# Gathering residual rows with their inverse root as a column, and building the expert lists in smaller groups

## The chip, the cores and the metric

The kernel runs on one core of one Trainium2 chip. The metric is device time in microseconds (us) of one execution, the median of several runs. Engines are named as the profile names them: PE (TensorE), DVE (VectorE), ACT (ScalarE), POOL (GpSimd), SP (SyncE, which here only issues transfers).

## What is computed

One layer of a hybrid decoder on 520 tokens (512 of a prompt and 8 of a decoding batch), width 2048, all in float32: an RMSNorm and an input projection, a state-space branch and a dilated attention branch, an output projection with a residual add, and then a hierarchical mixture of experts. The change touches only the last part:

```python
def _finish(x, z_ssm, o_attn, lp):
    ...
    x = x + mix @ lp['w_out']                 # called x2 in the kernel
    h = _rmsnorm(x, lp['g_ffn_norm'])
    y = _hier_moe(h.reshape(b * s, D_MODEL), ...)
    return x + y.reshape(b, s, D_MODEL)

def _hier_moe(h, w_rg, b_rg, w_re, b_re, w_g, w_u, w_d):
    # router: best of 4 groups, then the best 2 of its 8 experts
    ...
    def expert_block(args):
        rows, e = args
        xb = h_pad[rows]
        return (jax.nn.silu(xb @ w_g[e]) * (xb @ w_u[e])) @ w_d[e]
    ...
    out = jax.ops.segment_sum(contrib, tok_s, num_segments=t)
```

There are 32 experts with 3 weight matrices of 4 MB each, so 403 MB of weights are read by the expert stage alone. A last RMSNorm gives the output.

## The kernel before

All engines run one program each, written out by hand, with semaphores between them. The stages follow each other: projections, scan and attention (to 758 us), the output projection of 16 column tiles (758 to 996 us), the router with its lists (1003 to 1051 us), 32 experts (1051 to 2115 us), the last norm.

**Rows of x2.** After every four tiles of the output projection PE turns them into token rows, ACT copies these to the tile `x2row` and squares them for the norm, and SP stores them to the DRAM tensor `x2_rows` (`store_x2`). When the last tile is in, the square root and its reciprocal give the inverse root of each row (`row_rstd`). ACT then multiplies all five row tiles by it (L1078), SP stores them to a second DRAM tensor `h_rows` (L519), and POOL starts gathering rows for the experts from `h_rows` once all five stores have landed (`s_hst`).

**Routing.** DVE computes logits, the two experts of each token and, from PE's prefix sums (L799), each token's position in its expert's list. It ranks the experts by their token counts (L1545 to L1551: `key`, `place`, `turn_of`); experts 0 and 1 are always the first two. The six first in the order are "wide" (128 list slots), the others "narrow" (64); what doesn't fit goes into up to 16 overflow blocks. After the ranking DVE computes for every token its block and its slot (`posblk`, `rv16`). A one-hot comparison (`select`, L1612) and small fp16 matmuls on PE (`lists`, L812) turn these into the index lists `idx_g` and `idx_s`. There are seven groups of lists: `GROUPS` holds first block, last block and slots.

**Experts.** Six halves of weights (2 MB each: gate, up, gate, up, down, down) are loaded per expert into a ring of ten slots by SP, in order; they are counted here from 0, so expert i uses the halves 6i to 6i+5. Slots 8 and 9 lie in region `A`, which also holds x2 and then the scratch of the routing. For each expert PE does `gate_up`, then `turn_rows` (transposes of the next expert's gathered rows), `turn_act`, `down`. A slot is loaded again only when PE has used the half that lies in it:

```python
def load_next(n, e):

    if n >= NSLOT:
        i, j = divmod(n - NSLOT, 6)
        if j < 2:
            sp.wait_ge(s_half, i + 1)
        elif j < 4:
            sp.wait_ge(s_up, i + 1)
        elif j == 4:
            sp.wait_ge(s_dh, i + 1)
        else:
            sp.wait_ge(s_dn, 2 * i + 2)
    load_half(n % NSLOT, n % 6, e)
```

Here `s_half` counts the experts whose first gate and up halves are used, `s_up` those whose `gate_up` is done, `s_dh` the first down halves used, `s_dn` two for each `down`.

On PE the first three groups of lists stand ahead of expert 0, the other four between its `gate_up` and the turning of expert 1's rows. On SP the halves 0 to 3 are loaded during the output projection, 4 to 6 after it, 7 when the stores to `h_rows` have landed, and 8 when all lists are done (`s_idx`). POOL gathers the rows of expert i+2 when those of expert i have been turned, then scatters the result rows of expert i.

Of the kernel before, what the change touches and what calls it, by code (L numbers as in the profile page):

```python
# [24 lines left out]
P = 128  # L25
# [15 lines left out]
GROUPS = [(0, 6, CAP), (6, 15, SLIM), (15, 24, SLIM), (24, 32, SLIM), (32, 38, CAP), (38, 44, CAP), (44, 48, CAP)]  # L41
LISTG = 9
# [28 lines left out]
def build(nc, t):  # L71
    at = layout()
    ctx = ExitStack()
    with ctx:
# [17 lines left out]
        h_rows = dram("h_rows", (T, DM))  # L92
        x2_rows = dram("x2_rows", (T, DM))
# [80 lines left out]
        xrow = [view(ms + DM * j, DM) for j in range(2)]  # L174
        xtr = view(ms + 4096, 16 * CAP)
        actv = view(ms + 6144, 512)
        actt = view(ms + 6656, 4 * CAP)
        yrow = view(ms + 7168, DM)
# [63 lines left out]
        s_hr = sem("h_row_ready")  # L242
        s_x2st, s_hst = sem("x2_stored"), sem("h_stored")
        s_lg = sem("logits_psum")
        s_ra, s_rb = sem("router_act"), sem("router_dve")
        s_pos = sem("positions_psum")
        s_sel, s_lst, s_idx = sem("selection_ready"), sem("lists_psum"), sem("indices_ready")
# [35 lines left out]
        keep = Cols(ms + 7168 + DM)  # L283
        gate_w = keep(10).rearrange("p (t j) -> p t j", t=5)
        idx_g = keep(NBLK).bitcast(U32)
        idx_s = keep(NBLK).bitcast(U32)
        idx_now = keep(2).bitcast(U32)
# [4 lines left out]
        assert keep.at <= ring0, keep.at - ring0  # L292
        late = Cols(at["rstd"])
# [4 lines left out]
        rt = Cols(at["A"])  # L298
        SELN = 5 * 6 * CAP // 2
        sel_at = rt.at  # L300
        sel_v = [rt(SELN), rt(SELN), yrow[:, 0:SELN]]
        order_t = [view(sel_at + NE * NE * j, NE * NE).rearrange("p (a b) -> p a b", a=NE) for j in range(2)]

        def sel16(g):
            b0, b1, cap = GROUPS[g]
            n = 5 * (b1 - b0) * cap // 2
            return sel_v[g % 3][:, 0:n].bitcast(F16).rearrange("p (t b s) -> p t b s", t=5, b=b1 - b0)

        wide_at = rt.at
# [4 lines left out]
        wide_e = [view(wide_at, 320), view(wide_at + 320, 320), rt(320), rt(320)]  # L314
# [9 lines left out]
        none = rt(2 * LISTG)  # L324
# [50 lines left out]
        TURNED = [sum(TURNS[:i]) for i in range(NE + 1)]  # L375

# [7 lines left out]
        def _(sp):  # L384
# [87 lines left out]
            def store_x2(g):  # L472

                c = slice(512 * g, 512 * (g + 1))
                sp.wait_ge(s_trev, 5 * (g + 1))
                sp.dma_start(x2_rows[0:SEQ, c].rearrange("(i p) n -> p i n", p=P), x2row[:, 0:4, c]
                             ).then_inc(s_x2st, 16)
                sp.dma_start(x2_rows[SEQ:T, c], x2_of[4][0:NS, c]).then_inc(s_x2st, 16)

# [24 lines left out]
            for n in range(2, 16):  # L504
                if n % 4 == 3 and n > 4:
                    store_x2(n // 4 - 1)
# [4 lines left out]
            store_x2(3)  # L511
# [12 lines left out]
            for n in range(8, 12):  # L524
                load_next(n, 1)
            sp.wait_ge(s_ord, 1)
# [15 lines left out]
            for i, n in enumerate(TOKS):  # L542
                sp.dma_start(fx[i][0:n], x2_rows[P * i:P * i + n, :]).then_inc(s_finl[i], 16)
# [13 lines left out]
            sp.wait_ge(s_hst, 16 * 5)  # L557
# [3 lines left out]
        def _(pe):  # L561
# [242 lines left out]
            def lists(g):  # L804
# [3 lines left out]
                if g >= 3:  # L808
                    pe.wait_ge(s_idx, g - 2)
                for b in range(b1 - b0):  # L810
                    for i in range(5):
                        last = mm(ps[0:cap, 4 + g % 3, 2 * b:2 * b + 2], sel16(g)[:, i, b, :],  # L812
                                  rv16[:, i, b0 + b, :], start=(i == 0), stop=(i == 4))
                last.then_inc(s_lst, 1)

            def turn_rows(j, gathered, cap, turned):

                pe.wait_ge(s_gat[j], gathered)
                rows = xrow[j][0:cap, :].rearrange("p (m k) -> p k m", k=16)
# [71 lines left out]
            for g in range(3):  # L891
                lists(g)
            turn_rows(0, 16, CAP, 0)
            for i in range(NE):
                slots, uses = slots_of(i)
                gate_up(WIDE[i], slots, uses, TURNED[i + 1], i)
                if i == 0:
                    for g in range(3, len(GROUPS)):
                        lists(g)
                if i + 1 < NE:  # L900
                    turn_rows((i + 1) % 2, 16 * ((i + 1) // 2 + 1), CAP if WIDE[i + 1] else SLIM, TURNED[i + 1])
                turn_act(WIDE[i], i)
                if i == 0:
                    pe.wait_ge(s_idx, len(GROUPS))
                down(WIDE[i], slots, uses, i)

            def overflow_block(it):
                turned = it * 4 + TURNED[NE]
                turn_rows(0, it * 16 + 16 * (NE // 2 + 1), CAP, turned)
# [9 lines left out]
        def _(act):  # L919
# [143 lines left out]
            for b in range(20):  # L1063
# [52 lines left out]
        def _(pool):  # L1116
# [103 lines left out]
            pool.wait_ge(s_hst, 16 * 5)  # L1220
# [21 lines left out]
        def _(dve):  # L1242
# [246 lines left out]
            dve.wait_ge(s_rrs, 2)  # L1489
            dve.wait_ge(s_lg, 1)  # L1490
# [39 lines left out]
            p_, b_, w_, o_, id_, q_, f_, over_ = C10[0:8]  # L1530
# [3 lines left out]

            dve.wait_ge(s_pos, 1)
# [15 lines left out]
            dve.tensor_copy(ord_i, turn_of).then_inc(s_ord, 1)  # L1551
            link(ts(room, place, float(NWIDE), float(CAP - SLIM), ALU.is_lt, ALU.mult))
# [53 lines left out]
            def select(g):  # L1606
                b0, b1, cap = GROUPS[g]
                if g == 2:
                    dve.wait_ge(s_hst, 16 * 5)
                if g >= 3:  # L1610
                    dve.wait_ge(s_lst, g - 2)
                tt(sel16(g), iota_s[:, 0:cap].unsqueeze(1).unsqueeze(1).to_broadcast([P, 5, b1 - b0, cap]),  # L1612
                   posblk[:, :, b0:b1].unsqueeze(3).to_broadcast([P, 5, b1 - b0, cap]),
                   ALU.is_equal).then_inc(s_sel, 1)

            def lists(g):
# [221 lines left out]
```

## Time and profile before

| | |
|---|---|
| median of 3 runs | 2178.23 us (2176.87 to 2182.03) |
| the profiled execution | 2177.13 us, of which the profile's span is 2175.3 us |
| busy share of the span | PE 85%, DVE 27%, ACT 13%, POOL 12% |
| read from DRAM, written | 522.81 MB, 37.26 MB |
| mean granted TensorE clock | 0.933 |
| DMA engines busy, by fortieths of the span | 5143122257634034325199999999999999999947 |

Each digit of the last line is a tenth of busy time in a slice of 54 us: the transfers fill the expert stage, and there is a hole right before it. Times in the rows below are in us from the span's start, unless marked otherwise.

### The profile page before, as it was taken

The numbers are of one execution on the slowest core, as the hardware profiler recorded it, in microseconds if no ns is written. First come the engines' busy times: TensorE is split into PE (matmuls) and PEld (weight loads), VectorE is DVE, ScalarE is ACT, GpSimd is POOL, SyncE is SP. The second block draws the span as 40 slices with busy tenths as digits, with TensorE's granted clock in tenths as the row PEclk, the third lists the DMA queues.
The fourth block names the chain that finished last, engine by engine and source line by source line (L and its number), as shares of the span: only waits on it lengthen the run. The fifth ranks groups of instructions, "written<-read, shape, count | busy, mean of one in ns | idle before, by whom it ended". The sixth has DMA issues, their size and how long they took to land.

```text
span 2175.3 us, 22268 instructions
## 1 busy us (share of the span) xinstructions
PE 1848.2 (85%) x8916; PEld 1158.4 (53%) x8916; DVE 594.2 (27%) x1115; ACT 271.9 (13%) x535; POOL 270.6 (12%) x187
## 2 busy tenths in 40 slices
PE   7798999998789899994899896988979877877870
PEld 6687888886467688883443332433334332332320
DVE  6800799642144300005611111010110100100116
ACT  3001211004531101113000000000000000000002
POOL 0641222203900000000100000010000000000000
PEclk9899999999989999997799998999999998988995
DMA  5143122257634034325199999999999999999947
GB/s 222 59 135 98 65 77 77 104 197 137 4 137 178 36 116 170 122 78 214 53 400 397 392 409 408 407 412 393 398 412 386 391 413 406 411 400 406 399 203 295
DMA packets 91141, 544.85 MB, mean 250 GB/s; under 512 B 27984, under 2 KB 40784, under 8 KB 44400
## 3 DMA queue, kind: packets, MB, share of 16 engines
q1 hardware_dynamic: 70512, 520.24, 63.1%
q0 software_dynamic: 5888, 17.05, 2.3%
q10 hardware_dynamic: 14656, 6.33, 1.3%
q8 instruction: 64, 1.05, 0.2%
q14 instruction: 21, 0.17, 0.0%
HBM read 522.81 MB, written 37.26 MB: 257 GB/s over the span
## 4 chain that ended last, share of the span: by engine, by line
PE 58%; DMA 25%; DVE 9%; POOL 3%; ACT 2%; issue 1%; SPq 1%; ACTq 0%; POOLq 0%; DVEq 0%
PE psum L567 30%; DMA arena<-w_up_in 22%; PE psum L884 9%; PE psum L849 7%; PE psum L842 4%; PE psum L845 3%; PE psum L825 2%; DMA arena<-y_rows 1%; DMA arena<-v_cache_in 1%; DVE arena L1612 1%; SPq L484 1%; PE psum L729 1%; DVE arena L1709 1%; PE psum L765 1%; DVE arena L1450 1%
## 5 line engine op out<-in xcount | busy, mean ns | idle before, releaser
L567 PE MATMUL psum<-arena 128*128 128x260 f32 x3328 | 750.5, 389 | 40.3 <-ACT arena L930 13.4
L567 PEld LDWEIGHTS psum<-arena 128*128 128x128 f32 x3328 | 642.7, 194 | 144.1 <-issue 29.0
L849 PE MATMUL psum<-arena 128*64 128x512 f32 x832 | 402.5, 642 | 115.6 <-DMA arena<-w_up_in 115.6
L851 PE MATMUL psum<-arena 128*64 128x512 f32 x832 | 403.2, 643 | 0.0
L849 PEld LDWEIGHTS psum<-arena 128*64 128x64 f32 x832 | 119.5, 148 | 379.7 <-issue 379.7
L884 PE MATMUL psum<-arena 128*64 128x512 f32 (+1 forms) x1024 | 275.3, 606 | 17.7 <-ACT arena L1095 17.0
L884 PEld LDWEIGHTS psum<-arena 128*64 128x64 f32 (+1 forms) x1024 | 95.6, 149 | 174.8 <-issue 152.7
L1210 POOL DMA_INDIRECT y_rows<-arena x32 | 30.0, 938 | 998.3 <-DVE arena L1686 998.3
L1677 DVE TENSOR_TENSOR arena<-arena,psum 64x512 f32<-64x512 f32 x26 | 18.0, 691 | 495.4 <-ACT arena L1092 495.4
L1686 DVE COPY arena<-psum 64x512 f32<-64x512 f32 (+1 forms) x64 | 43.5, 687 | 280.6 <-PE psum L884 279.8
L851 PEld LDWEIGHTS psum<-arena 128*64 128x64 f32 x832 | 119.5, 148 | 0.0
L842 PE MATMUL psum<-arena 128*128 128x512 f32 x192 | 86.6, 604 | 4.9 <-DMA arena<-w_up_in 4.1
L845 PE MATMUL psum<-arena 128*128 128x512 f32 x192 | 84.4, 592 | 0.0
L1092 ACT ACTIVATE arena<-psum 64x512 f32<-64x512 f32 x26 | 15.3, 589 | 511.2 <-PE psum L849 511.2
L825 PEld LDWEIGHTS psum<-arena 64*128 64x128 f32 (+1 forms) x512 | 62.6, 204 | 30.2 <-issue 24.1
L825 PE MATMUL psum<-arena 64*128 64x64 f32 (+1 forms) x512 | 69.6, 287 | 4.2 <-DVE arena L1634 4.0
L1483 DVE TENSOR_TENSOR arena<-psum,arena 128x520 f32<-128x520 f32 x16 | 11.2, 700 | 223.0 <-PE psum L567 223.0
L1355 DVE TENSOR_TENSOR arena<-arena 128x64 f32<-128x64 f32 x128 | 46.3, 361 | 92.7 <-ACT arena L959 82.3
L1101 ACT ACTIVATE arena<-psum 64x512 f32<-64x512 f32 (+1 forms) x64 | 37.3, 593 | 248.4 <-PE psum L884 247.7
L842 PEld LDWEIGHTS psum<-arena 128*128 128x128 f32 x192 | 36.6, 193 | 53.4 <-issue 52.2
L845 PEld LDWEIGHTS psum<-arena 128*128 128x128 f32 x192 | 36.5, 190 | 45.9 <-issue 45.9
L1222 POOL MEMSET arena<- 128x2048 f32 x2 | 3.5, 1804 | 436.1 <-DMA h_rows<-arena 436.1
(309 smaller groups left out, 1348.2 us busy)
## 6 DMA issues: line engine op xcount, KB each, us to landing
arena<-w_gate_in SPq DMA_DIRECT2D x64, 2048.0 KB, 38.2
arena<-w_up_in SPq DMA_DIRECT2D x64, 2048.0 KB, 42.3
arena<-w_down_in SPq DMA_DIRECT2D x64, 2048.0 KB, 41.6
arena<-w_in_in SPq DMA_DIRECT2D x32, 1024.0 KB, 4.8
arena<-w_out_in SPq DMA_DIRECT2D x16, 1024.0 KB, 4.8
arena<-k_cache_in SPq DMA_DIRECT2D x8, 1024.0 KB, 6.8
arena<-v_cache_in SPq DMA_DIRECT2D x8, 1024.0 KB, 4.8
arena<-y_rows SPq DMA_DIRECT2D x4, 2048.0 KB, 19.3
```

What stands on the lines that cost most here:

```text
L484: sp.dma_start(half_gu(slot), src[:, 8 * (j // 2):8 * (j // 2) + 8, :]).then_inc(s_ring[slot], 16)
L567: last = mm(pair(n)[:, h, :], w(kk), rhs(kk)[:, HALF * h:HALF * (h + 1)], start=(kk == 0), stop=(kk == kn - 1 and stop))
L825: last = pe.transpose(ps[:, g % 2, cap * m:cap * (m + 1)], rows[:, per * g + m, :], ident[0:cap, 0:cap])
L842: lastg = mm(ps[:, 2, :], xt[:, 8 * hf + kk, :], wg[:, kk, :], start=(hf == 0 and kk == 0), stop=(hf == 1 and kk == 7))
L845: lastu = mm(ps[:, 3, :], xt[:, 8 * hf + kk, :], wu[:, kk, :], start=(hf == 0 and kk == 0), stop=(hf == 1 and kk == 7))
L849: lastg = mm(ps[0:SLIM, 2, :], xt[:, 8 * hf + kk, :], wg[:, kk, :], start=(hf == 0 and kk == 0), stop=(hf == 1 and kk == 7))
L851: lastu = mm(ps[SLIM:P, 2, :], xt[:, 8 * hf + kk, :], wu[:, kk, :], start=(hf == 0 and kk == 0), stop=(hf == 1 and kk == 7))
L884: last = mm(out, at_[:, kk, :], wd[:, kk - 2 * hf, 512 * c:512 * (c + 1)], start=(kk == 0), stop=(kk == 3))
L1101: A(yrow[0:cap, 512 * c:512 * (c + 1)], src, ACT.Copy).then_inc(s_ya, 1)
L1210: pool.indirect_dma_start(out=y_rows, out_offset=bass.IndirectOffsetOnAxis(ap=index, axis=0), in_=yrow[0:cap, :], in_offset=None, bounds_c ...
L1355: tt(scan_t[:, 0], column(it * 4 + s), lam_same, ALU.mult).then_inc(s_scan, 1)
L1686: dve.tensor_copy(yrow[0:cap, 512 * c:512 * (c + 1)], src).then_inc(s_yd, 1)
```

## The change

- `h_rows`, ACT's multiplication and SP's five stores go. `x2_rows` gets 16 more columns (`ROWW` = 2064), all holding the row's inverse root: DVE spreads it over 16 columns, ACT stores them in five small transfers. POOL gathers rows of 2064 from `x2_rows`, and DVE multiplies the gathered rows by their last column (`scale_rows`) ahead of the turning.
- The stores of x2 move from SP to ACT.
- On SP the halves 4 to 8 wait until all stores have landed; half 8 no longer waits for the lists. The halves 10 and 11 go ahead of 9; half 9 waits until the routing's scratch is free (`s_free`).
- The scratch of the routing moves into the slot of half 9; lists and list scratch that live longer move elsewhere.
- The lists of experts 0 and 1 (a group of its own, blocks 0 to 1) are made ahead of the ranking. The ranking, expert 0's scaling and the turning of its rows follow; the rest of the routing comes behind those on DVE. Two more groups (`EARLY` = 3 in all) are made into lists on PE and DVE after expert 0's `gate_up`, behind the turning of expert 1's rows; the other 25 groups (two narrow blocks or one overflow block each) are made two at a time behind the first 13 experts.

```diff
-GROUPS = [(0, 6, CAP), (6, 15, SLIM), (15, 24, SLIM), (24, 32, SLIM), (32, 38, CAP), (38, 44, CAP), (44, 48, CAP)]
+EARLY = 3
+GROUPS = ([(0, 2, CAP), (6, 15, SLIM), (2, 6, CAP)] + [(b, min(b + 2, NE), SLIM) for b in range(15, NE, 2)]
+          + [(b, b + 1, CAP) for b in range(NE, NBLK)])
+ROWW = DM + 16
...
-        h_rows = dram("h_rows", (T, DM))
-        x2_rows = dram("x2_rows", (T, DM))
+        x2_rows = dram("x2_rows", (T, ROWW))
...
+        LATE = (len(GROUPS) - EARLY + 1) // 2
...
             sp.wait_ge(s_op, 16)
+            sp.wait_ge(s_x2st, 16 * 8)
+            sp.wait_ge(s_rst, 16 * 5)
             for n in range(4, 6):
                 load_next(n, 0)
             load_next(6, 1)
-            for i, n in enumerate(TOKS):
-                sp.wait_ge(s_hr, i + 1)
-                sp.dma_start(h_rows[P * i:P * i + n, :], x2_of[i][0:n]).then_inc(s_hst, 16)
-            sp.dma_start(gtab, t["g_ffn"].rearrange("o (p k) -> (o p) k", k=16)).then_inc(s_gt, 16)
-            sp.wait_ge(s_hst, 16 * 5)
+            sp.wait_ge(s_rss, 20)
             load_next(7, 1)
-            sp.wait_ge(s_idx, len(GROUPS))
-            for n in range(8, 12):
+            sp.wait_ge(s_lg, 1)
+            load_next(8, 1)
+            for n in (10, 11):
                 load_next(n, 1)
+            sp.wait_ge(s_free, 1)
+            load_next(9, 1)
             sp.wait_ge(s_ord, 1)
...
+            def late_lists(i):
+                for g in range(EARLY + 2 * i, min(EARLY + 2 * i + 2, len(GROUPS))):
+                    lists(g, ps[:, 0, 8 * (g % 2):8 * (g % 2) + 8])
...
-                pe.wait_ge(s_gat[j], gathered)
+                pe.wait_ge(s_sr, scaled)
...
-            for g in range(3):
-                lists(g)
-            turn_rows(0, 16, CAP, 0)
+            lists(0, ps[:, 4, :])
+            turn_rows(0, 1, CAP, 0)
             for i in range(NE):
                 slots, uses = slots_of(i)
                 gate_up(WIDE[i], slots, uses, TURNED[i + 1], i)
+                if i + 1 < NE:
+                    if 1 <= i <= LATE:
+                        pe.wait_ge(s_idx, min(EARLY + 2 * i, len(GROUPS)))
+                    turn_rows((i + 1) % 2, i + 2, CAP if WIDE[i + 1] else SLIM, TURNED[i + 1])
                 if i == 0:
-                    for g in range(3, len(GROUPS)):
-                        lists(g)
-                if i + 1 < NE:
-                    turn_rows((i + 1) % 2, 16 * ((i + 1) // 2 + 1), CAP if WIDE[i + 1] else SLIM, TURNED[i + 1])
+                    for g in range(1, EARLY):
+                        lists(g, ps[:, 4 + g, :])
                 turn_act(WIDE[i], i)
                 if i == 0:
-                    pe.wait_ge(s_idx, len(GROUPS))
+                    pe.wait_ge(s_idx, EARLY)
                 down(WIDE[i], slots, uses, i)
+                if i < LATE:
+                    if i + 1 < NE:
+                        pe.wait_ge(s_xte, TURNED[i + 2])
+                    late_lists(i)
...
+                if i == 4:
+                    c = slice(512 * g, 512 * (g + 1))
+                    act.dma_start(x2_rows[0:SEQ, c].rearrange("(i p) n -> p i n", p=P), x2row[:, 0:4, c]
+                                  ).then_inc(s_x2st, 16)
+                    act.dma_start(x2_rows[SEQ:T, c], x2_of[4][0:NS, c]).then_inc(s_x2st, 16)
...
-            act.wait_ge(s_rrs, 2)
-            act.wait_ge(s_x2st, 16 * 8)
+            act.wait_ge(s_rsc, 1)
             for i, n in enumerate(TOKS):
-                A(x2_of[i][0:n], x2_of[i][0:n], ACT.Copy, scale=row_rstd[0:n, i:i + 1]).then_inc(s_hr, 1)
+                act.dma_start(x2_rows[P * i:P * i + n, DM:ROWW], rstd_cols[0:n, i, :]).then_inc(s_rst, 16)
...
-                    out=xrow[j][0:cap, :], out_offset=None, in_=h_rows,
+                    out=xrow[j][0:cap, :], out_offset=None, in_=x2_rows,
...
-            pool.wait_ge(s_hst, 16 * 5)
+            pool.wait_ge(s_x2st, 16 * 8)
+            pool.wait_ge(s_rst, 16 * 5)
...
+            dve.tensor_copy(rstd_cols, row_rstd.unsqueeze(2).to_broadcast([P, 5, 16])).then_inc(s_rsc, 1)
...
+            tt(two(first_a), hot1[:, :, 0:2], full(id_[:, 0:5], 2), ALU.mult)
+            link(tt(two(first_b), hot2[:, :, 0:2], full(id_[:, 5:10], 2), ALU.mult))
+            tt(rv16[:, :, 0:2, 0:1], two(first_a).unsqueeze(3), two(first_b).unsqueeze(3), ALU.add)
+            link(dve.tensor_copy(rv16[:, :, 0:2, 1:2], full(tok1, 2).unsqueeze(3)))
...
             dve.wait_ge(s_pos, 1)
+            link(stt(posblk[:, :, 0:2], ps[:, 1, 0:160].rearrange("p (t e) -> p t e", t=5)[:, :, 0:2], 1.0,
+                     m16[:, :, 0:2], ALU.add, ALU.mult))
+            select(0)
             link(dve.tensor_copy(rank, ps[:, 1, 0:160].rearrange("p (t e) -> p t e", t=5)))
             link(dve.tensor_copy(cnt, ps[:, 1, 160:192]))
+            lists(0, ps[:, 4, :])
+            dve.wait_ge(s_x2st, 16 * 8)
...
             dve.tensor_copy(ord_i, turn_of).then_inc(s_ord, 1)
...
+            def scale_rows(j, gathered, cap):
+                dve.wait_ge(s_gat[j], gathered)
+                ts(xrow[j][0:cap, 0:DM], xrow[j][0:cap, 0:DM], xrow[j][0:cap, DM:DM + 1], None, ALU.mult
+                   ).then_inc(s_sr, 1)
+
+            dve.wait_ge(s_gt, 16)
+            scale_rows(0, 16, CAP)
+            rows_turned(CAP, 0)
             link(ts(room, place, float(NWIDE), float(CAP - SLIM), ALU.is_lt, ALU.mult))
...
-            select(0)
-            lists(0)
             select(1)
-            select(2)
-            lists(1)
-            lists(2)
-            dve.wait_ge(s_gt, 16)
-            rows_turned(CAP, 0)
-
             dve.wait_ge(s_ra, 4)
...
-            for g in range(3, len(GROUPS)):
+            select(2)
+            for g in range(EARLY, EARLY + 2):
                 select(g)
-                if g >= 5:
-                    lists(g - 2)
-            for g in range(len(GROUPS) - 2, len(GROUPS)):
-                lists(g)
...
             for i in range(NE):
+                if i + 1 < NE:
+                    scale_rows((i + 1) % 2, 16 * ((i + 1) // 2 + 1), CAP if WIDE[i + 1] else SLIM)
                 gated(i, WIDE[i])
                 if i + 1 < NE:
                     rows_turned(CAP if WIDE[i + 1] else SLIM, TURNED[i + 1])
+                if i == 0:
+                    for g in range(1, EARLY):
+                        lists(g, ps[:, 4 + g, :])
+                    dve.sem_inc(s_free, 1)
                 rows_out(i, WIDE[i])
+                if i < LATE:
+                    dve.wait_ge(s_lst, min(EARLY + 2 * i + 2, len(GROUPS)))
+                for g in range(EARLY + 2 * i, min(EARLY + 2 * i + 2, len(GROUPS))):
+                    lists(g, ps[:, 0, 8 * (g % 2):8 * (g % 2) + 8])
+                for g in range(EARLY + 2 * i + 2, min(EARLY + 2 * i + 4, len(GROUPS))):
+                    select(g)
```

## Rows read from the trace of the kernel before

**Rows 1.** Busy time by stretch: instructions in brackets, granted clock, DMA share, GB/s.

```profile
1003.00:1037.00 34.00, 2.92 (x63) 2.58 (x63) 29.19 (x82) 13.87 (x13) 2.47 (x2) 0.51 0.90 354
...
1042.00:1087.00 45.00, 41.88 (x278) 24.23 (x278) 25.72 (x41) 0.60 (x1) 3.46 (x2) 0.84 0.07 16
...
1087.00:2107.00 1020.00, 877.13 (x3597) 354.52 (x3595) 110.98 (x166) 67.99 (x125) 57.08 (x60) 0.94 0.98 395
```

**Rows 2.** The chain that ended last, in order of time, its last wait for weights.

```profile
2055.40 42.16 DMA arena<-w_up_in
```

**Rows 3.** SP's issues in order of time: start, length, line, destination and source.

```profile
1004.18 1.80 SPq L487 DMA_DIRECT2D arena<-w_down_in  x2
...
1010.62 7.86 SPq L519 DMA_DIRECT2D h_rows<-arena  x5
...
1034.50 0.33 SPq L484 DMA_DIRECT2D arena<-w_up_in  x1
1086.64 0.33 SPq L484 DMA_DIRECT2D arena<-w_gate_in  x1
...
1152.22 0.33 SPq L484 DMA_DIRECT2D arena<-w_up_in  x1
1159.25 0.95 SPq L487 DMA_DIRECT2D arena<-w_down_in  x2
```

**Rows 4.** All engines in order of time, from the router to expert 0.

```profile
1008.59 9.57 ACT L1078 ACTIVATE arena<-arena 128x2048 f32<-128x2048 f32 x5 [4.01 <-DMA x_rows<-arena]
...
1012.31 0.32 DVE L1528 TENSOR_TENSOR arena<-arena 128x160 f16<-128x160 f32 x1
...
1020.70 0.17 DVE L1552 TENSOR_SCALAR arena<-arena 128x32 f32<-128x32 f32 x1
...
1031.96 4.16 DVE L1612 TENSOR_TENSOR arena<-arena 128x3840 f16<-128x3840 f32 x1
...
1034.53 3.54 POOL L1222 MEMSET arena<- 128x2048 f32 x2 [436.12 <-DMA h_rows<-arena]
...
1037.53 0.15 DVE L1624 SCALAR_TENSOR_TENSOR arena<-psum,arena 128x6 uint32<-128x6 f32 x1
...
1039.09 2.90 POOL L1201 DMA_INDIRECT arena<-h_rows,arena  x1 [1.01 <-issue]
...
1040.93 2.56 PE L812 MATMUL psum<-arena 128*64 128x2 f16 x45 [3.72 <-DVE arena L1612]
...
1046.49 3.97 PE L825 MATMUL psum<-arena 128*128 128x128 f32 x16
...
1051.24 8.80 PE L842 MATMUL psum<-arena 128*128 128x512 f32 x16 [0.78 <-DVE arena L1634]
...
1056.25 10.96 DVE L1612 TENSOR_TENSOR arena<-arena 128x2560 f16<-128x2560 f32 x3
```

**Rows 5.** PE after expert 0's gate and up products, in order of time.

```profile
1080.57 3.01 PE L812 MATMUL psum<-arena 128*64 128x2 f16 x100
...
1091.55 15.97 PE L884 MATMUL psum<-arena 128*128 128x512 f32 x32 [0.73 <-issue]
```

**Rows 6.** The 32 gathers: duration on POOL and landing, each as minimum, median and maximum.

```profile
L1201 POOL DMA_INDIRECT arena<-h_rows,arena x32: 949/955/2905, 1039.1 to 2027.9; - x32
...
DMA to landing us min/median/max: 5.2/11.9/17.1
```

**Rows 7.** Landing of single transfers: gather 0, half 8 (issued 1086.64), half 22 (1159.25).

```profile
arena<-h_rows,arena POOLq DMA_INDIRECT x1, 6.1
...
arena<-w_gate_in SPq DMA_DIRECT2D x1, 2048.0 KB, 7.4
...
arena<-w_down_in SPq DMA_DIRECT2D x1, 2048.0 KB, 15.1
```

**Rows 8.** DVE by line and shape: busy, mean ns of one.

```profile
L1612 DVE TENSOR_TENSOR arena<-arena 128x2880 f16<-128x2880 f32 x2 | 6.2, 3154 | 0.0
...
L1285 DVE TENSOR_SCALAR arena<-arena 128x1056 f32<-128x1056 f32 x1 | 0.7, 709 | 0.0
```

More of the change, by code:

```diff
@@ L172, in build @@
         ro_at = at["cos"]
[L174 to L178, printed above, removed]
+        xrow = [view(ms + ROWW * j, ROWW) for j in range(2)]
+        xtr = view(ms + 2 * ROWW, 16 * CAP)
+        actv = view(ms + 2 * ROWW + 2048, 512)
+        actt = view(ms + 2 * ROWW + 2560, 4 * CAP)
+        yrow_at = ms + 2 * ROWW + 3072
+        yrow = view(yrow_at, DM)
         ring = [ring0 + HALFW * j for j in (4, 5, 6, 7, 1, 2, 3, 0)] + [at["A"], at["A"] + HALFW]
@@ L296, in build @@
         assert late.at <= at["cos"]
[L298 to L302, printed above, removed]
+        none = stat[:, 44:62]
+        rstd_cols = region("lr", 80).rearrange("p (t c) -> p t c", t=5)
+        late_sel = [view(ro_at + 30, 320), region("lr", 320)]
+        rt = Cols(at["A"] + HALFW)
+        scratch_at = rt.at
+        order_t = [yrow[:, NE * NE * j:NE * NE * (j + 1)].rearrange("p (a b) -> p a b", a=NE) for j in range(2)]
+        early_sel = [view(scratch_at, 640), yrow[:, 0:1440], view(scratch_at, 1280)]
         def sel16(g):
@@ L556, in _ @@
             sp.wait_ge(s_vout, 16)
-            sp.wait_ge(s_hst, 16 * 5)
+            sp.wait_ge(s_x2st, 16 * 8)
+            sp.wait_ge(s_rst, 16 * 5)
         @block.tensor
@@ L1533, in _, with two, select, lists @@
             link(ts(tok1, tok, 1.0, None, ALU.add))
+            def two(ap):
+                return ap.rearrange("p (t b) -> p t b", t=5)
+            tt(two(first_a), hot1[:, :, 0:2], full(id_[:, 0:5], 2), ALU.mult)
+            link(tt(two(first_b), hot2[:, :, 0:2], full(id_[:, 5:10], 2), ALU.mult))
+            tt(rv16[:, :, 0:2, 0:1], two(first_a).unsqueeze(3), two(first_b).unsqueeze(3), ALU.add)
+            link(dve.tensor_copy(rv16[:, :, 0:2, 1:2], full(tok1, 2).unsqueeze(3)))
+            def select(g):
+                b0, b1, cap = GROUPS[g]
+                if g >= EARLY + 2:
+                    dve.wait_ge(s_lst, g - 1)
+                tt(sel16(g), iota_s[:, 0:cap].unsqueeze(1).unsqueeze(1).to_broadcast([P, 5, b1 - b0, cap]),
+                   posblk[:, :, b0:b1].unsqueeze(3).to_broadcast([P, 5, b1 - b0, cap]),
+                   ALU.is_equal).then_inc(s_sel, 1)
+            def lists(g, out):
+                b0, b1, cap = GROUPS[g]
+                dve.wait_ge(s_lst, g + 1)
+                src = out[0:cap, 0:2 * (b1 - b0)].rearrange("p (b c) -> p b c", c=2)
+                no = none[0:cap, 0:2 * (b1 - b0)].rearrange("p (b c) -> p b c", c=2)
+                link(ts(no, src, 0.0, BIG, ALU.is_equal, ALU.mult))
+                stt(idx_s[0:cap, b0:b1].unsqueeze(2), src[:, :, 0:1], -1.0, no[:, :, 0:1],
+                    ALU.add, ALU.add)
+                stt(idx_g[0:cap, b0:b1].unsqueeze(2), src[:, :, 1:2], -1.0, no[:, :, 1:2],
+                    ALU.add, ALU.add).then_inc(s_idx, 1)
+                dve.wait_ge(s_idx, g + 1)
             dve.wait_ge(s_pos, 1)
+            link(stt(posblk[:, :, 0:2], ps[:, 1, 0:160].rearrange("p (t e) -> p t e", t=5)[:, :, 0:2], 1.0,
+                     m16[:, :, 0:2], ALU.add, ALU.mult))
+            select(0)
             link(dve.tensor_copy(rank, ps[:, 1, 0:160].rearrange("p (t e) -> p t e", t=5)))
             link(dve.tensor_copy(cnt, ps[:, 1, 160:192]))
+            lists(0, ps[:, 4, :])
+            dve.wait_ge(s_x2st, 16 * 8)
             def across(ap):
@@ L1551, in _, with rows_turned @@
             dve.tensor_copy(ord_i, turn_of).then_inc(s_ord, 1)
+            def rows_turned(cap, turned):
+                per = 512 // cap
+                xt = xtr[:, 0:16 * cap].rearrange("p (k n) -> p k n", k=16)
+                for g in range(16 // per):
+                    dve.wait_ge(s_xt, turned + (g + 1))
+                    tt(xt[:, per * g:per * (g + 1), :], ps[:, g % 2, :].rearrange("p (k n) -> p k n", n=cap),
+                       gtab[:, per * g:per * (g + 1)].unsqueeze(2).to_broadcast([P, per, cap]), ALU.mult
+                       ).then_inc(s_xte, 1)
+            def scale_rows(j, gathered, cap):
[5 more added lines that the diff above has]
+            rows_turned(CAP, 0)
             link(ts(room, place, float(NWIDE), float(CAP - SLIM), ALU.is_lt, ALU.mult))
```

81 lines of the change are left out of this document (23 added, 58 removed).

## Prediction

> **What bounds the kernel now.** I read the page's busy slices first, then the stretches, the chain, SP's issues and the order of work around the router. The slices show transfers filling the second half of the span with a hole before it. The stretches give both sizes: from 1087 to 2107 us the DMA engines are busy 0.98 of the time, and from 1042 to 1087 they are busy 0.07 of it [rows 1]. The chain says the same from the other end: its last wait for weights is 42.16 us long and ends at 2097.6 [rows 2]. So the expert stage is a stream of 192 halves that has no slack: halves 8 to 189, 182 of them, land between 1086.64 [rows 3] and 2097.6, 5.55 us each, 33 us an expert. Its end moves only if the stream gets ahead earlier, or if each expert costs the stream something else.
>
> SP's issues tell why it starts so late. Halves 4 to 6 go out at 1004 to 1006, half 7 only at 1034.50, when the `h_rows` stores have landed, half 8 at 1086.64, when all lists are done [rows 3]. POOL's memset began at 1034.53 for the same reason, and expert 0 at 1051.24 [rows 4]. But the hole of 45 us is not the gain to be had. A ring of ten slots lets halves 16 and later go only as PE frees them, so after the hole the stream can't run ahead of PE. I look for the place where both meet: half 22 (expert 3's first down half), issued at 1159.25 when expert 2's first half was used, and landed 15.1 us later, at 1174.4 [rows 3, 7]. A half with nothing ahead of it took 7.4 us [rows 7], so 7.7 us of that were queue: there the stream was behind PE, and it stays full to the end.
>
> **The change part by part.** Times after are on the scale of the trace before.
>
> *Stores and root column.* ACT's two issues for the last rows stand ahead of the square root. An issue on SP took 0.33 us [rows 3]; for ACT I take 0.5, of which the old wait for DVE's sum hides a part: 0.8 us. DVE's copy into 16 columns is a short operation, 0.2. The selected experts (`m16`), ready at 1012.6 before [rows 4], come at 1013.6. Between none and twice these prices lies 1 us to either side.
>
> *List 0.* Seven short DVE operations, four of them new, and the position read follow, at 0.17 us [rows 4] and a gap 0.2 each, with PE's sums beside them: 1015.2. The selection has 2 x 5 x 128 = 1280 elements; 3840 took 4.16 us [rows 4], so 1.4: 1016.6. PE's 10 matmuls, where 45 took 2.56 [rows 4], 0.6; three DVE operations, 0.6: list 0 at 1017.8. Before, the first list ended at 1037.68 and the gather started at 1039.09 [rows 4], 1.4 later: 1019.2. On ACT only the two exponentials for the gates stand behind the new issues, and DVE reads those after expert 0 has started. The stores don't hold the gather: those of x2 landed at 1008.6 before [rows 4], the five root columns some 3 us later, and POOL's memset of 3.54 [rows 4] then ends near 1015.5.
>
> *Gather 0.* Before, it took 6.1 us beside the end of one half [rows 7], of which POOL's first issue was 2.9 where the others took 0.96 [rows 6]. Now SP sends the halves 4 to 8 once the stores have landed, near 1011.5, five times some 5 us, until about 1037, so the gather meets them. Under the full stream the 32 gathers had a median of 11.9 and a maximum of 17.1 [rows 6]. I take the median and the longer first issue, 11.9 + 1.9 = 13.8: it lands at 1033.0. The ends are 6.1 (1025.3) and 17.1 + 1.9 (1038.2).
>
> *Scaling and turning.* One DVE operation of 2048 elements; 1056 took 0.71 [rows 8], so at most 1.4; I take 1.3. The lower end is the 0.7 of half as many elements, the upper the pace of the selection in the same rows, 2.2. PE's turning up to expert 0's first product took 1046.49 to 1051.24 [rows 4], 4.75. Expert 0 starts at 1039.1 instead of 1051.24: **12.1 us earlier**.
>
> *What waits behind it on DVE.* The scaling stands in DVE's queue ahead of the rest of the routing, 1020.70 to 1031.96 = 11.3 us [rows 4]; select 1, 3.15 [rows 8]; gates and overflow, 1051.24 to 1056.25 = 5.0 [rows 4]; select 2, 2.8; two of 640 elements, 1.4; expert 1's scaling, 1.3. Together 25 us, hidden behind expert 0's gate and up products, 1051.24 to 1080.57 = 29.3 [rows 4, 5]. Cover of 4 us is left; beyond it each us of DVE holds expert 1's turning by one.
>
> *After expert 0's products.* Before, PE came to the down product 11.0 us after them [rows 5], waiting for selections. Now: turning 4.0 [rows 4], lists of 45 and 20 matmuls 2.6 + 1.1, the turning of the activations a quarter of 4.0, ACT's copy 0.6: 9.3, so 1.7 gained. Each later pair of lists is 20 matmuls, 1.1 us on PE; two pairs stand before expert 2. Expert 2 starts 12.1 + 1.7 - 2.3 = **11.5 us earlier**. The remaining pairs fall into experts that wait for weights, and cost nothing while they do.
>
> *The halves.* Half 8 leaves early; 10 and 11 wait for expert 0's first half; 9 waits behind them on SP for the scratch, near 1077, with 12 and 13 right after it. All three are there by about 1094, and half 9 is needed in the middle of expert 1, after 1107. From 14 on PE sets the issues: during two wide experts pairs of halves, 10 us of stream, go out every 14 us or so, so the queue runs empty. Half 21, issued at 1152.22 before [rows 3], goes 12.7 earlier, at 1139.5, and lands 7.4 later, before half 22 is issued at 1159.25 - 11.5 = 1147.8. What half 22 can still meet is expert 1's scatter and gather. With none of the old queue it lands 11.5 + 7.7 = 19.2 earlier, with all of it 11.5; since only one expert's row transfers stand there, for which I allow 2 us, I take **17**.
>
> *The rest of the stream* is as full as before, so the 17 us last to the end. DVE's scalings of later experts wait for gathers, but a gather is issued about an expert (33 us) ahead and lands 17.1 at the latest [rows 6]. They stand ahead of `gated`, which waits for PE's whole product anyway. The tail after the last weights is untouched.
>
> The profiled execution took 2177.13 (span 2175.3), 1.1 under the median. So 2177.1 - 17 = 2160.1 on its scale, **2161 us** as a median.
>
> **Rivals.** *Gather 0 lands as on an empty queue* (it has few rows and goes out while the halves have just begun): 1025.3, the start 7.7 earlier still, gain 24.7, 2153.5. For it: its own 6.1 before; against: five halves in flight, and the median of 11.9 among full queues [rows 6].
>
> *The early start is taken back: the gather waits out the halves sent ahead of it.* Before, the gather started with one half in flight; now with five. If it landed only after all of them, near 1039 to 1045, expert 0 would start at 1045 to 1051 and the gain be 11 to 5: 2167 to 2173. It decides from a landing at 1045, 26 us after issue. Against it: of the 32 gathers, nearly all in the full stream, none took over 17.1 [rows 6]. The Trainium skill (DMA: Bandwidth & Descriptors, "Queues, rings and completion order") says that each DMA engine takes turns between queues packet by packet; by that rule the gather would not wait out the halves, and the trace's 17.1 agrees.
>
> *Slower: each expert costs the full stream more.* Rows are 64 bytes longer and no longer start at a multiple of 8 KB, and DVE now works 1.3 us per expert on the tile that POOL's gathers fill. With no slack in the stream, 17 us over 30 experts is gone at 0.57 us an expert; at the whole 1.3 us it would be 39 - 17 = 22 slower, 2199. Against it: the bytes grow by 0.8% of the gathers, and the weights, nearly all of the stream, are issued by SP, not POOL. The Trainium skill (SBUF — State Buffer, "SBUF: two separate sides") warns of this: an fp32 copy-like DVE operation in a two-port mode locks GpSimd out of its SBUF port, so that descriptors of POOL's transfers are written only after it. By that rule up to 1.3 us per expert would be added to a gather; no run here shows whether the stream feels it.
>
> **How the numbers follow.** The forecast has 0.58, with its own range from 2155 to 2168 (landing of the gather 5.2 either way, queue 2). The empty-queue rival has 0.12, the lost start 0.16, the slower one 0.10; 0.04 is left for what I don't see. The range runs from 2150, a few us below the empty-queue case, to 2173, the worst of the lost start, and leaves the slower case out. A measurement of this kernel tells 0.3%, 6.5 us, from no change: under 2171.7 is faster. That takes the first two and three quarters of the lost start: 0.82. The rest of it, and part of the unseen, is the same: 0.08. Slower 0.10.
>
> **What would show it.** In the profile after: expert 0's first product near 1039 (right if 1033 to 1045); gather 0's landing 14 us after its start; the DMA share between 1042 and 1087 well over 0.07; half 22 issued near 1148 and landing within 10 us; the stretch from half 22 to the last weights as long as before. The prediction is wrong if that stretch grows, by 0.57 us an expert or more, if DVE's routing ends after expert 0's products, or if expert 0 starts after 1051.

## The result and the profile after

The changed kernel takes **2150.07 us** (median of 4 runs, 2146.59 to 2152.12) against 2177.77 of the kernel before beside it (4 runs, 2176.87 to 2182.03). The ratio is 0.9871, 95% interval 0.9859 to 0.9884: 27.7 us faster. The forecast was 2161, a gain of 17: the direction was right, the size was not. The time lies outside the forecast's own range (2155 to 2168) and on the edge of the whole one (2150 to 2173).

The profiled execution took 2152.12 us, its span 2150.5. One thing has to be settled before its rows are set beside those of before. The position sums of PE, up to which both kernels do nearly the same work, stand at different times:

```profile
1012.69 0.72 PE L799 MATMUL psum<-arena 128*128 128x32 f16 x20 [8.22 <-DVE arena L1528]
```

(the kernel before, PE in order of time), and after:

```profile
1015.79 0.72 PE L798 MATMUL psum<-arena 128*128 128x32 f16 x20 [8.43 <-DVE arena L1541]
```

Of the 3.1 us, 2.8 are older than the change: the output projection's first matmuls begin at 758.15 before and at 760.91 here, and in the nine profiled executions of this kernel and those below, whose code is the same up to there, at 757.5 to 762.8. From there to the sums it is 254.5 us before and 254.7 to 254.9 in the nine, so what the change adds ahead of the sums costs at most 0.3. So times below are compared **after the sums**, as distances from these two rows and their like. On that scale the profiled execution is 24.8 + 3.1 = 27.9 us shorter, as the medians say.

The stretches, with the columns of [rows 1]:

```profile
1012.00:1037.00 25.00, 4.54 (x45) 3.91 (x46) 16.15 (x37) 1.88 (x4) 6.97 (x4) 0.50 0.98 399
1042.00:1087.00 45.00, 43.71 (x169) 21.32 (x168) 23.90 (x53) 1.19 (x2) 0.95 (x1) 0.92 0.57 213
1087.00:2070.00 983.00, 855.88 (x3682) 348.75 (x3680) 169.83 (x288) 66.45 (x122) 71.46 (x60) 0.94 0.99 398
```

The hole of 45 us, 0.07 busy before [rows 1], is now 0.57 busy, and the stream behind it is as full as it was. SP's issues tell which halves fill it (4 to 8 go out at 1011.79 to 1014.19, then 10 and 11 together, 9, and half 22):

```profile
1052.19 0.89 SPq L485 DMA_DIRECT2D arena<-w_down_in  x2
1071.38 0.34 SPq L482 DMA_DIRECT2D arena<-w_up_in  x1
...
1142.28 1.50 SPq L485 DMA_DIRECT2D arena<-w_down_in  x2
```

All engines from list 0 to expert 0's down product, which answer to [rows 4, 5]:

```profile
1011.82 3.57 POOL L1234 MEMSET arena<- 128x2064 f32 x2 [410.32 <-DMA x_rows<-arena]
...
1016.82 1.49 DVE L1561 TENSOR_TENSOR arena<-arena 128x1280 f16<-128x1280 f32 x1
...
1019.24 0.15 DVE L1573 SCALAR_TENSOR_TENSOR arena<-psum,arena 128x2 uint32<-128x2 f32 x1
...
1020.38 1.63 POOL L1212 DMA_INDIRECT arena<-x_rows,arena  x1 [4.99 <-DVE arena L1573]
...
1032.24 1.29 DVE L1612 TENSOR_SCALAR arena<-arena 128x2048 f32<-128x2048 f32 x1 [6.12 <-DMA arena<-x_rows,arena]
1033.58 3.80 PE L827 MATMUL psum<-arena 128*128 128x128 f32 x16 [14.72 <-DVE arena L1612]
1038.16 7.13 PE L844 MATMUL psum<-arena 128*128 128x512 f32 x16 [0.79 <-DVE arena L1606]
...
1065.73 1.06 PE L827 MATMUL psum<-arena 128*128 128x128 f32 x8
1067.35 1.31 PE L827 MATMUL psum<-arena 128*128 128x128 f32 x8 [0.55 <-DVE arena L1606]
1068.59 2.17 PE L809 MATMUL psum<-arena 128*64 128x2 f16 x65
1071.99 17.02 PE L886 MATMUL psum<-arena 128*128 128x512 f32 x32 [0.73 <-DVE arena L1573]
```

Expert 0 begins 22.37 us after the sums, before 1051.24 - 1012.69 = 38.55: 16.2 us earlier. And the landings, gather 0 and half 22, which answer to [rows 7]:

```profile
arena<-x_rows,arena POOLq DMA_INDIRECT x1, 11.8
...
arena<-w_down_in SPq DMA_DIRECT2D x1, 2048.0 KB, 9.3
```

Half 22 is issued 126.49 us after the sums (before 146.56) and lands at 135.79 (before 161.66): 25.9 us earlier. The last transfer of weights in the chain,

```profile
2030.58 40.44 DMA arena<-w_up_in
```

ends at 2030.58 + 40.44 = 2071.02, 1055.2 after the sums, where [rows 2] give 1084.9: 29.6 us earlier. The tail is 1.8 us longer (79.5 against 77.7).

### The profile page after: what moved, and what is told of

Its sections match the earlier page's. It is cut to its first block, busy times and chain, and to the rows that moved or that the text cites. A ratio compares the mean times of both kernels' runs of the same rounds, so it can differ in the third digit from the quotient of the medians.

```text
span 2150.5 us, 22432 instructions
## 1 busy us (share of the span) xinstructions
PE 1849.8 (86%) x8916; PEld 1159.5 (54%) x8916; DVE 644.2 (30%) x1237; ACT 262.4 (12%) x530; POOL 283.1 (13%) x187
## 4 chain that ended last, share of the span: by engine, by line
PE 61%; DMA 23%; DVE 8%; POOL 3%; ACT 2%; issue 1%; SPq 1%; ACTq 0%; POOLq 0%; DVEq 0%
PE psum L566 30%; DMA arena<-w_up_in 20%; PE psum L886 9%; PE psum L851 6%; PE psum L844 4%; PE psum L847 4%; PE psum L853 2%; PE psum L827 2%; DMA arena<-y_rows 1%; DMA arena<-v_cache_in 1%; SPq L482 1%; PE psum L728 1%; DMA arena<-x_rows,arena 1%; DVE arena L1746 1%; PE psum L764 1%
## 5 line engine op out<-in xcount | busy, mean ns | idle before, releaser
L1221 POOL DMA_INDIRECT y_rows<-arena x32 | 36.6, 1144 | 939.0 <-DVE arena L1710 611.5
```

The lines of the kernel that those rows point to most:

```text
L1221: pool.indirect_dma_start(out=y_rows, out_offset=bass.IndirectOffsetOnAxis(ap=index, axis=0), in_=yrow[0:cap, :], in_offset=None, bounds_c ...
```

## The experiments

Three theories were at stake. The *start* (A): the end follows from when expert 0 begins. The *early fill* (B): it follows from the halves that get into the hole. The *ring* (C), formed after the first four runs: a slot is free only when PE has used it, so the stream runs just so far ahead of PE; expert 0's start sets when PE's slots come free, the early halves decide how much has piled up by then, and what fits into the hole costs nothing. C has a gauge, the prediction's own: where half 22 lands, its issue (PE) plus the queue that it meets (halves sent late). Each kernel is the changed one with the edit shown (`...` marks lines left out), and computes all of the reference. Gains are (1 - ratio) x 2177; the ratios' intervals leave 3 to 6 us to either side.

**Scaling on ACT.**

```diff
-            scale_rows(0, 16, CAP)                     # DVE, and one ahead of each gated()
+                act.wait_ge(s_gat[j], gathered)        # ACT, ahead of each expert()
+                A(xrow[j][0:cap, 0:DM], xrow[j][0:cap, 0:DM], ACT.Copy, scale=xrow[j][0:cap, DM:DM + 1]
+                  ).then_inc(s_sr, 1)
```

> The changed kernel, but the gathered rows are multiplied by their root column on ACT instead of DVE. My theory: DVE's scaling does lengthen POOL's issues (mean 1.21 us against 0.97 before), but the stream of weights does not feel it. POOL's gathers go back to about 0.97 us; ACT's operation takes about 2.0 us instead of DVE's 1.3, so expert 0 starts about 0.7 us later; the end stays within 2 us of the changed kernel (2149 to 2152 us). Rival: the lock costs the full stream what it costs POOL, 0.24 us a gather and 0.19 us a scatter over some 28 experts, 12 us; then this kernel is 8 to 12 us faster than the changed one, near 2140 us.

2149.41 us, ratio 0.9864 [0.984, 0.9888]: no difference from the changed kernel; the interval ends at 6.7 us faster, short of the rival's 8 to 12. POOL's gathers and scatters, by line from 1087 us on, were lengthened by DVE's scaling and are nearly not so here. The changed kernel:

```profile
L1221 POOL DMA_INDIRECT y_rows<-arena x32 | 36.6, 1144 | 939.0 <-DVE arena L1710 611.5 <-DVE arena L1573 327.5
L1212 POOL DMA_INDIRECT arena<-x_rows,arena x29 | 35.7, 1232 | 8.8 <-issue 8.8
```

and with the scaling on ACT:

```profile
L1234 POOL DMA_INDIRECT y_rows<-arena x32 | 32.5, 1016 | 949.4 <-DVE arena L1717 613.9 <-DVE arena L1586 335.6
L1225 POOL DMA_INDIRECT arena<-x_rows,arena x29 | 29.5, 1018 | 8.8 <-issue 8.8
```

Before, the same rows had a mean of 939 and 964 ns. So DVE's scaling does lengthen POOL's issues, by some 0.2 us in the mean (12 of the 29 gathers take 1.4 to 1.7 us, the others 0.95 to 1.03 as before), and the full stream does not feel it. Whether a port is what they share was not tried.

**Halves 8, 10 and 11 wait with 9 for the scratch.**

```diff
-            load_next(8, 1)
-            for n in (10, 11):
-                load_next(n, 1)
             sp.wait_ge(s_free, 1)
-            load_next(9, 1)
+            for n in range(8, 12):
+                load_next(n, 1)
```

> The changed kernel, but the halves 8, 10 and 11 wait with 9 until the routing's scratch is free (as they waited for the lists before); nothing else moves. Theory A: the end follows PE's start of expert 2, since halves from 16 on are issued as PE frees slots; three halves more, 15 us of stream, are waiting at 1071 us, but the stream has gaps of some 10 us between there and half 22, so half 22 lands 4 to 6 us later and the end is 4 to 6 us later, 2154 to 2156 us; expert 0 to 2 start as in the changed kernel. Theory B: the gain comes from loading into the hole, so three halves fewer at that point cost 15 us: 2165 us.

2165.91 us, ratio 0.9933 [0.9908, 0.9958]: about half the gain is gone. Expert 0 begins 22.15 us after the sums and half 22 is issued 126.36 after them, both as in the changed kernel,

```profile
1012.34 0.72 PE L796 MATMUL psum<-arena 128*128 128x32 f16 x20 [8.40 <-DVE arena L1539]
...
1034.49 7.13 PE L842 MATMUL psum<-arena 128*128 128x512 f32 x16 [0.78 <-DVE arena L1604]
```

but half 22 lands 18.1 us after its issue, not 9.3:

```profile
arena<-w_down_in SPq DMA_DIRECT2D x1, 2048.0 KB, 18.1
```

A falls: PE ran alike, and the end came 13.5 us later, where A had 4 to 6. B is near, with 13.5 of its 15 us.

**Halves 4 to 6 ahead of the wait for the stores.**

```diff
-            sp.wait_ge(s_x2st, 16 * 8)
-            sp.wait_ge(s_rst, 16 * 5)
             for n in range(4, 6):
                 load_next(n, 0)
             load_next(6, 1)
+            sp.wait_ge(s_x2st, 16 * 8)
+            sp.wait_ge(s_rst, 16 * 5)
```

> The changed kernel, but the halves 4 to 6 are issued as soon as the output projection is done, ahead of the stores' landing, as before; 7 and 8 still wait for the stores. Theory A (end follows PE's start): the five root columns now share the DMA engines with 6 MB of weights and land 3 to 12 us later; POOL's memset and gather 0 follow if they land after 1017 us, and the gather itself meets one or two halves less; expert 0 starts 0 to 8 us later and the end moves by as much: 2150 to 2158 us. Theory B (early fill of the ring decides): halves 4 to 8 are in 5 to 7 us earlier, the end is the same or earlier by up to 5 us: 2145 to 2150 us.

2156.16 us, ratio 0.989 [0.9862, 0.9917]: some 4 us slower than the changed kernel, though the two intervals overlap. That is within A's 2150 to 2158 and above B's 2145 to 2150. The halves don't help by being early; they hold up the stores, and with them POOL:

```profile
1021.43 3.57 POOL L1234 MEMSET arena<- 128x2064 f32 x2 [420.97 <-DMA x_rows<-arena]
```

That is 6.6 us after the sums, where the changed kernel's memset stands 4.0 before them. Expert 0 begins 3.5 us later than there.

**List 0 behind the ranking and the routing.**

```diff
-            select(0)                       # with its four operations, right behind the sums
-            lists(0, ps[:, 4, :])
...
-            dve.wait_ge(s_gt, 16)           # right behind the ranking
-            scale_rows(0, 16, CAP)
-            rows_turned(CAP, 0)
...
+            select(0)                       # behind the ranking and the routing
+            lists(0, ps[:, 4, :])
             select(1)
+            dve.wait_ge(s_gt, 16)
+            scale_rows(0, 16, CAP)
+            rows_turned(CAP, 0)
```

> The changed kernel, but the list of experts 0 and 1 is made after the ranking and the whole routing, as before; root column, stores, early halves and late lists stay. Theory A (end follows PE's start): list 0 comes 18 to 20 us later, near 1040 us instead of 1019; the gather then finds few halves in flight and lands in 6 to 8 us; expert 0 starts 14 to 17 us later than in the changed kernel, near 1053 us, and the end comes 14 to 17 us later: 2164 to 2167 us. Theory B (early fill decides): half 8 is loaded as early as in the changed kernel and only 9 to 11 are late, so no more than 5 us are lost: 2150 to 2155 us.

2164.6 us, ratio 0.9933 [0.9907, 0.9958]. Here A is right and B falls: expert 0 begins 35.62 us after the sums,

```profile
1012.77 0.71 PE L798 MATMUL psum<-arena 128*128 128x32 f16 x20 [8.38 <-DVE arena L1541]
...
1048.39 7.13 PE L844 MATMUL psum<-arena 128*128 128x512 f32 x16 [0.78 <-DVE arena L1593]
```

13.2 us later than in the changed kernel, and the end comes 13.5 later. So each theory explains one of the two runs and fails at the other. That is where C comes from.

**Halves 4 to 8 wait for gather 0.**

```diff
             sp.wait_ge(s_rst, 16 * 5)
+            sp.wait_ge(s_gat[0], 16)
             for n in range(4, 6):
```

> SP holds the halves 4 to 8 until gather 0 has landed, so the gather meets no weights. It took 11.8 us among them; beside the end of one half it took 6.1, so expert 0 should start some 5.7 us earlier, and so should everything that PE releases (halves 10 and 11, then 9, 12 and 13, down to half 22). The halves 4 to 8 are sent some 15 us later, into a hole of the stream that the ring leaves open anyway. Theory C (the ring lets the stream run only so far ahead of PE; transfers that fit into the hole cost nothing): about 5.5 us faster than the changed kernel, 2143 to 2146. Rival (what counts is how early the first halves are in): 2150 to 2158, as the stream has moved nothing for 15 us.

2142.67 us, ratio 0.984 [0.9825, 0.9854]: 6.8 us faster than the changed kernel, the best version of all; C's range was 2143 to 2146, its rival's 2150 to 2158. Its gather 0:

```profile
arena<-x_rows,arena POOLq DMA_INDIRECT x1, 5.0
```

and its engines in order of time:

```profile
1024.29 0.89 SPq L485 DMA_DIRECT2D arena<-w_down_in  x2
1024.78 0.18 DVE L1599 CAST arena<-arena 128x32 uint32<-128x32 f32 x1
1024.87 1.28 DVE L1613 TENSOR_SCALAR arena<-arena 128x2048 f32<-128x2048 f32 x1
...
1030.61 7.13 PE L845 MATMUL psum<-arena 128*128 128x512 f32 x16 [0.89 <-DVE arena L1607]
```

Alone, the gather lands in 5.0 us instead of 11.8; expert 0 begins 6.4 us earlier and the end comes 6.8 earlier, though SP's five halves go out 13.7 us later (9.7 us after the sums, against 4.0 ahead of them). Little more is to be had this way: the rows are in at 1024.2, and the scaling follows the ranking, which ends at 1024.96, without a gap.

**Two stores of 2 MB put back, behind half 8.**

```diff
             load_next(8, 1)
+            for j in (2, 3):
+                sp.wait_ge(s_ring[j], 16)
+                sp.dma_start(extra[P * (j - 2):P * (j - 1), :], view(ring[j], HALFW)).then_inc(s_ext, 16)
             for n in (10, 11):
...
             load_next(9, 1)
+            sp.wait_ge(s_ext, 32)
```

> Two extra stores of 2 MB each (4.2 MB, as much as the five stores to the second row tensor that the change removed) go out on SP behind half 8; nothing but the loads of halves 12 and 13 waits for them. At the stream's 395 GB/s they are 10.6 us of DMA time. Theory C (they fall into the hole of some 15 us between half 8 and half 10): 0 to 2 us, 2150 to 2152. Rival (the stream is one sum of bytes, so the removed stores are 10.6 us of the 27.7 gained): 2158 to 2161.

2150.07 us, ratio 0.9871 [0.9854, 0.9887]: no difference, as C had it. In the stretch after half 8 the DMA engines, busy 0.27 in the changed kernel,

```profile
1036.00:1046.00 10.00, 9.21 (x26) 4.44 (x25) 8.77 (x33) 0.00 (x0) 0.00 (x0) 0.94 0.27 114
```

are busy 0.99 with the extra stores:

```profile
1034.50:1044.50 10.00, 9.22 (x25) 4.40 (x24) 8.69 (x33) 0.00 (x0) 0.00 (x0) 0.93 0.99 401
```

So 4 MB more cost nothing where the stream has a hole. (The stores that the change removed stood elsewhere, ahead of gather 0; what their absence is worth, the last run tells.)

**Halves 10 and 11 behind 9.**

```diff
-            for n in (10, 11):
-                load_next(n, 1)
             sp.wait_ge(s_free, 1)
-            load_next(9, 1)
+            for n in range(9, 12):
+                load_next(n, 1)
```

> The halves 10 and 11 wait with half 9 for the routing's scratch again, so they go out at about 1071 instead of 1052; half 8 stays early, PE's work is untouched. PE theory (the end follows from expert 0's start): 2150. Theory C: two halves, 11.1 us of stream, leave the hole; the holes of some 6 us that the changed kernel's stream still has between 1087 and 1140 are filled by them, so about 5 us slower, 2154 to 2157. Rival (all of the two halves is lost): 11 us, 2161.

2158.03 us, ratio 0.9903 [0.9886, 0.9921], 7.0 us slower than the changed kernel by the ratios: at the upper edge of what C gives (4 to 7; the median lies 1 us above its range) and less than the rival's 11. Half 22 lands 13.8 us after its issue.

**List 0 late and the halves held, together.**

The edits of the second and the fourth run, together.

> Both at once: list 0 is made behind the ranking and the routing (expert 0 starts 13.3 us later, 13.6 us slower by itself), and half 8 is held together with 10, 11 and 9 (13.5 us slower by itself, with expert 0's start as in the changed kernel). What is left of the change is the missing second store of rows and the lists behind the experts. Theory C (with the halves held, the stream is full from the moment the scratch comes free, and that moment moves with expert 0): the two losses add up, 2176 to 2180, the kernel before. Rival (each is a bound by itself and the later one sets the end): 2165 to 2168. Rival (stores and later lists are worth something by themselves, some 10 us): 2168 to 2172.

2177.48 us (12 runs), ratio 1.0 [0.9986, 1.0013]: the whole gain is gone. 13.5 and 13.5 add up to 27.0, and 28.1 were lost. So the missing second tensor of rows, the lists behind the experts and the scaling on DVE bring nothing by themselves, within 3 us and taken together (effects that cancel are not excluded); they are what lets list 0 and the halves go early. (Its profiled execution is 7.4 us shorter after the sums than that of before, which the ratio does not bear out; single executions differ by several us.)

The gauge for all kernels: expert 0's start and half 22's issue in us after the sums, the time from that issue to the landing, and by how much the landing is earlier than before (advance), beside the measured gain:

| kernel | expert 0 | half 22 issued | landing | advance | gain |
|---|---|---|---|---|---|
| before | 38.55 | 146.56 | 15.1 | | |
| changed | 22.37 | 126.49 | 9.3 | 25.9 | 28.1 |
| scaling on ACT | 22.77 | 126.80 | 9.6 | 25.3 | 29.6 |
| halves held | 22.15 | 126.36 | 18.1 | 17.2 | 14.6 |
| halves first | 25.90 | 129.94 | 9.5 | 22.2 | 23.9 |
| list late | 35.62 | 139.92 | 9.5 | 12.2 | 14.6 |
| gather 0 first | 15.98 | 120.02 | 9.2 | 32.4 | 34.8 |
| stores back | 22.20 | 126.41 | 9.6 | 25.7 | 28.1 |
| 10, 11 behind 9 | 21.71 | 126.15 | 13.8 | 21.7 | 21.1 |
| late and held | 35.44 | 139.86 | 17.6 | 4.2 | 0.0 |

From 0 to 34.8 us the gain follows the landing of one half within some 4 us. Neither the start alone nor the queue alone does that: the kernels "halves held" and "list late" have one gain at starts 13.5 us apart. What is left over has a pattern. Where half 8 goes out early PE first waits for weights 274 to 305 us after the sums, and where it is late (before, "halves held", "late and held") 197 to 214. So the place where PE and the stream meet moves too, and half 22 is a near gauge, not that place itself.

## Why the prediction was right in direction and wrong in size

**What bounds it** was right, and so was the place to look. The runs bear out that the end moves as half 22's landing does, by PE's issue and by the queue.

**The step that failed** is "Expert 2 starts 12.1 + 1.7 - 2.3 = 11.5 us earlier", read there as half 22's issue. It went out 146.56 - 126.49 = 20.1 us earlier. The 8.6 us have two parts.

*Expert 0's start* was sized 12.1 and was 16.2. By the prediction's stations, the gather was to start 6.5 us after the sums and started 4.6 after them: of the 1.0 us ahead of the sums for ACT's issues and DVE's copy at most 0.3 came, the chain of list 0 was 0.5 shorter, and the gather left POOL 1.0 us after its list, not 1.4. It was to take 13.8 and took 11.8: the median of 11.9 was right, and the 1.9 added for a long first issue on POOL was not needed (1.63 us, not 2.9). The scaling (1.29 against 1.3) and the turning (4.6 against 4.75) were near.

*From expert 0's start to half 22's issue* the prediction had a loss, 1.7 - 2.3 = -0.6. It was 108.0 before and is 104.1, a gain of 3.9. These were mostly prices read at the wrong clock. The turning "4.0 [rows 4]", the 45 matmuls of the lists "2.6 [rows 4]" and the first three us of the products all come from a stretch at a granted clock of 0.50, the lower of the two levels. The turning before:

```profile
1046.00:1051.00 5.00, 4.43 (x27) 3.57 (x25) 2.98 (x7) 0.00 (x0) 0.00 (x0) 0.50 0.02 5
```

In the changed kernel the same work after expert 0's products runs at 1.00 (the stretch 1038 to 1070 in the last section). There the turning of expert 1's rows takes from 1065.73 to 1068.66, the lists of 65 matmuls 2.17 (the 100 of [rows 5], 3.01 us, had told that pace), and the down product comes 6.3 us after the products, not 9.3: 3.0. Expert 0's products take 27.6, not 29.3: 1.8. A pair of late lists takes 0.79, not 1.1, twice: 0.6. The down product costs 17.0, not 16.0, as more of it runs at the lower level (0.82 in the mean over it, 0.87 before): 1.0 lost. Together 4.4 of the 4.5.

**The queue at half 22** was right: 15.1 - 9.3 = 5.8 us gone, against 7.7 - 2 = 5.7. Half 21 landed 8.1 us after its issue at 1134.62, just behind half 22's issue at 1142.28, and expert 1's scatter and the gather behind it were in flight, as forecast. **"As full as before, so the 17 us last to the end"** was right but for 3.8 us more: half 22 is not quite the place where the two meet. The changed kernel's PE runs ahead of its weights for longer. Its first wait for them,

```profile
1306.97 1.09 PE L851 MATMUL psum<-arena 128*64 128x512 f32 x1 [4.22 <-DMA arena<-w_up_in]
```

answers to one much earlier in the kernel before:

```profile
1226.72 7.10 PE L842 MATMUL psum<-arena 128*128 128x512 f32 x16 [2.70 <-DMA arena<-w_up_in]
```

**"The tail is untouched"**: 1.8 us longer. In sum 17.2 (not rounded to 17) + 4.0 + 4.5 + 0.1 + 3.8 - 1.8 = 27.8, the 27.9 of the traces. The misses that counted lay on one side. (The forecast's own range should have begun at 2154: 5.2 and 2 below 2161.)

**The cover on DVE** held: the work behind expert 0's scaling took the 25 us forecast and ended with expert 1's scaling at 1063.0, 2.7 us ahead of the end of the products. Forecast were 4; the products took 1.8 less. **The rivals.** Gather 0 on an empty queue was not what happened (11.8 us), though the measured time lies nearest to that rival's 2153.5: by the time alone the wrong cause would have been picked. Its price was near: when made so, the gather landed in 5.0 us and gave 6.8 more (7.7 forecast). The gather didn't wait out the halves: half 8, last of the five, landed 27.5 us after its issue, the gather after 11.8. The Trainium skill (DMA: Bandwidth & Descriptors, "Queues, rings and completion order") has each DMA engine take turns between queues packet by packet; that agrees. Costs per expert didn't arise. The Trainium skill (SBUF — State Buffer, "SBUF: two separate sides") warns that a DVE operation in a two-port mode holds up the descriptors of POOL's transfers. The rows show POOL's issues longer by some 0.2 us in the mean, and by the run with the scaling on ACT the kernel's time does not feel that.

## What to carry to other kernels

A ring whose slots are released by the consumer has two levers, when the consumer begins and what is already in the ring, and both must be moved: undoing either cost half of the gain here, undoing both all of it. In a hole that the ring leaves open anyway, transfers could be delayed (five halves by 13.7 us) or added (4.2 MB) at no cost; so let the small transfer that the consumer waits for go first, and the large ones after it. A price read from a row has the clock of its stretch: look at the granted clock there, and at the one that the work will have at its new place.

## What the runs showed of the hardware

Beside a full queue, two kinds of small transfers fared differently, and their packets differ; no run changed the packets alone. In the run with the halves first, from 1006 to 1012 us, the queue of the halves and ACT's queue had these shares of the DMA engines' time (queue: packets, MB, share):

```profile
q1 hardware_dynamic: 262, 2.36, 93.9%
q10 hardware_dynamic: 115, 0.24, 10.1%
```

That is some 9 KB a packet against 2 KB. ACT's queue moved 0.24 MB in 6 us, and the last store of x2 (1 MB) with the five of the root columns (8 KB or less) released POOL 10.6 us later than in the changed kernel. The gather beside the halves, with rows of 8 KB, went from 5.0 only to 11.8.

The granted clock was at the lower of its two levels (0.50, 1.2 GHz) while PE waited for the rows of expert 0 and turned them, and at its upper one (1.00, 2.4 GHz) as expert 0's products ran (the stretches before, around and behind its start, changed kernel):

```profile
1030.00:1037.00 7.00, 3.42 (x15) 2.96 (x16) 3.03 (x4) 0.00 (x0) 0.00 (x0) 0.50 1.00 418
...
1038.00:1070.00 32.00, 31.29 (x124) 15.60 (x125) 26.79 (x60) 0.60 (x1) 0.00 (x0) 1.00 0.36 140
1070.00:1078.00 8.00, 7.27 (x37) 3.52 (x35) 0.80 (x6) 0.60 (x1) 0.95 (x1) 0.58 0.76 255
```

Before, expert 0's first three us ran at the lower level too, though PE had been busy for 4.4 of the 5 us ahead of them (1046 to 1051):

```profile
1051.00:1054.00 3.00, 2.76 (x4) 1.21 (x5) 2.73 (x10) 0.00 (x0) 0.95 (x1) 0.50 0.32 66
```

So the same 16 matmuls took 7.13 us here and 8.80 before [rows 4]. Why the clock rose just before the products here and 3 us into them before was not tried.
